# Experts three to thirty-two in an order made on the chip from the token counts, with weight addresses from a table

## The reference, cut to what matters

```python
logits = xt @ w_router + b_router            # 264 tokens, 32 experts
top_val, top_idx = lax.top_k(logits, 4)      # four experts a token
gates = softmax(top_val)
counts = bincount(top_idx)                   # 1056 assignments over 32 experts
for each expert e, each block of its tokens:
    gu  = xb @ w_gate_up[e] + b_gate_up[e]   # 1024 x 2048 weights, 8 MB
    act = (clip(lin) + 1) * min(glu, 7) * sigmoid(1.702 * glu)
    y  += gate * (act @ w_down[e] + b_down[e])   # 1024 x 1024 weights, 4 MB
```

## Time and profile before

| | us |
|---|---|
| median of 3 runs | 1265.24 (1260.77 to 1265.37) |
| profiled execution, first to last instruction (its span) | 1258.5 |
| what lies around the span, median less span | 6.7 |
| PE matmuls busy | 1102.0 (88%) |
| DVE busy | 588.2 (47%) |
| ACT busy | 230.7 (18%) |
| POOL busy | 68.5 (5%) |
| moved by DMA | 485.30 MB, mean 386 GB/s |

### The profile page before, as it was taken

The page is one execution under the profiler, slowest core; times in us unless marked ns, Lnnn a source line. Parts: engine busy times, 40 slices in busy tenths (PEclk is TensorE's granted clock), DMA queues, the critical chain, the costliest instruction groups (busy, mean ns, idle before and its releaser), DMA issues.

```text
span 1258.5 us, 23992 instructions
## 1 busy us (share of the span) xinstructions
PE 1102.0 (88%) x9856; PEld 456.6 (36%) x9856; DVE 588.2 (47%) x1166; ACT 230.7 (18%) x420; POOL 68.5 (5%) x126
## 2 busy tenths in 40 slices
PE   8999999999988697996887979999966995667996
PEld 4776777785322131321222322333211331112332
DVE  3536744444654252563353544666532552332654
ACT  3002510141311110220111211112100211100212
POOL 0312020250100000000000000000000000000000
PEclk9999999999989897998798999999988998888999
DMA  9979994599899999999999999999999999999995
GB/s 342 312 245 347 317 339 154 187 384 366 284 428 429 426 429 426 429 425 429 426 428 428 428 426 393 409 424 427 428 427 428 427 426 430 424 431 425 428 428 236
DMA packets 67619, 485.30 MB, mean 386 GB/s; under 512 B 6421, under 2 KB 29450, under 8 KB 40762
## 3 DMA queue, kind: packets, MB, share of 16 engines
q1 hardware_dynamic: 59312, 461.07, 88.9%
q0 software_dynamic: 7104, 19.65, 4.9%
q10 hardware_dynamic: 1130, 3.51, 0.8%
HBM read 479.47 MB, written 4.72 MB: 385 GB/s over the span
## 4 chain that ended last, share of the span: by engine, by line
DMA 45%; PE 27%; DVE 1%; issue 0%; DVEq 0%; ACT 0%; ACTq 0%
DMA big<-in_w_down 26%; PE PB L1247 13%; DMA big<-in_w_gate_up 13%; PE PB L1274 7%; DMA hTG<-in_w_down 5%; PE PB L1214 2%; PE PB L1201 2%; PE PB L1206 1%; PE PB L1229 1%; PE PB L1221 1%; PE PB L1240 0%; PE PB L1186 0%; PE PB L1232 0%; DVE big L1623 0%; DVE big L1620 0%
## 5 line engine op out<-in xcount | busy, mean ns | idle before, releaser
L1247 PE MATMUL PB<-big,cst 128*32 128x512 f32 x2768 | 355.0, 657 | 109.2 <-DMA big<-in_w_gate_up 109.2
L2189 DVE TENSOR_TENSOR tok<-PB,cst 32x512 f32<-32x512 f32 x188 | 129.1, 687 | 261.7 <-ACT cst L1554 259.8
L1247 PEld LDWEIGHTS PB<-big,cst 128*32 128x32 f32 x2768 | 89.0, 115 | 345.2 <-issue 181.1
L1274 PE MATMUL PB<-big,cst 128*32 128x512 f32 x1408 | 166.6, 602 | 12.8 <-DMA big<-in_w_down 12.7
L2165 DVE TENSOR_SCALAR mod<-PB 64x256 f32<-64x256 f32 x96 | 41.0, 427 | 209.1 <-PE PB L1247 208.4
L756 PE MATMUL PB<-hTG,big 128*128 128x264 f32 x576 | 136.5, 391 | 0.4 <-DVE hTG L1617 0.4
L756 PEld LDWEIGHTS PB<-hTG,big 128*128 128x128 f32 x576 | 106.9, 190 | 27.3 <-issue 10.8
L1544 ACT ACTIVATE mod<-PB 64x256 f32<-64x256 f32 x96 | 36.1, 376 | 422.3 <-PE PB L1247 421.7
L1274 PEld LDWEIGHTS PB<-big,cst 128*32 128x32 f32 x1408 | 39.2, 110 | 96.8 <-issue 65.8
L1201 PE MATMUL PB<-wide,att 128*32 128x256 f32 x784 | 57.9, 415 | 5.1 <-DVE att L2159 4.9
L1554 ACT ACTIVATE cst<-PB 128x512 f32<-128x512 f32 x48 | 28.7, 597 | 178.2 <-PE PB L1274 178.2
(11 more groups left out here) (378 smaller groups left out, 970.9 us busy)
## 6 DMA issues: line engine op xcount, KB each, us to landing
big<-in_w_gate_up SPq DMA_DIRECT2D x115, 2048.0 KB, 31.0
big<-in_w_down SPq DMA_DIRECT2D x57, 2048.0 KB, 23.9
hTG<-in_w_gate_up SPq DMA_DIRECT2D x13, 2048.0 KB, 37.1
big<-in_w_mod SPq DMA_DIRECT2D x24, 1024.0 KB, 7.5
big<-in_w_in SPq DMA_DIRECT2D x22, 1024.0 KB, 9.2
hTG<-in_w_down SPq DMA_DIRECT2D x6, 2048.0 KB, 24.0
wide<-in_cache_k POOLq DMA_DIRECT2D x16, 256.0 KB, 6.8
big<-in_w_out SPq DMA_DIRECT2D x4, 1024.0 KB, 10.5
```

Of the source, the lines that this page charges most:

```text
L1247: mm = pe.matmul(GU[32 * j:32 * j + 32, :], mo["xT"][:, (2 * u + r) * M:(2 * u + r + 1) * M], groups(w[:, r * 2 * D:(r + 1) * 2 * D])[:, j ...
L1274: mm = pe.matmul(DN[32 * j:32 * j + 32, :], mo["actT"][:, (4 * u + r) * M:(4 * u + r + 1) * M], w[:, r * D + half * 512:r * D + (half + 1) ...
L2189: mm = dve.tensor_tensor(mo["y"][rows, :], DN[rows, :], mo["y_part"][other, :], ALU.add)
```

## The change

Experts 0 and 1 stay first. After them the experts are taken in an order which DVE computes: ranked by number of blocks, ties by index, and placed heaviest, lightest, second heaviest, second lightest, and so on (constant `ranks`: 0, 1, 2, 31, 3, 30, ..., 16, 17). `tab` and `used_tab` are rewritten for that order from the third place on, `sel` has its columns exchanged, and the table `order` gives SP the expert at each place. The steps on DVE go ahead of the computation of places. A new semaphore `order_ready` holds SP before unit 12 and PE before the third place. From unit 12 on, SP's transfers take their source address from a register.

```diff
+    pairs = np.stack([np.arange(2, E // 2 + 1), E + 1 - np.arange(2, E // 2 + 1)], 1).reshape(-1)
+    put("ranks", np.tile(np.concatenate([[0, 1], pairs]), (P, 1)))
...
-        tab = sb("tab", [1, E + 2], I32)
-        used_tab = sb("used_tab", [1, E], I32)
+        tables = sb("tables", [33, E + 2], I32)
+        tab, used_tab = tables[0:1, :], tables[32:33, 0:E]
+        order = sb("order", [1, E], I32)
...
+            def load_unit(n, e=None):
+                src = unit_rows(n, slice(n // NU, n // NU + 1) if e is None else bass.ds(e, 1))
                 sp.dma_start(unit_slot(n), src).then_inc(unit_landed(n)[0], 16)
...
             for n in range(NSLOT, NLOAD):
                 e, u = (n - NSLOT) // NU, (n - NSLOT) % NU
+                if n > NSLOT and u == 0:
+                    sp.wait_ge(S("order_ready"), 1)
                 if n == NSLOT or u == 0:
                     before = sp.value_load(used_tab[0:1, e:e + 1], min_val=0, max_val=NU * MAXB)
+                if n // NU >= 2 and n % NU == 0:
+                    sp.wait_ge(S("order_ready"), 1)
+                    expert = sp.value_load(order[0:1, n // NU:n // NU + 1], min_val=0, max_val=E - 1)
                 sp.wait_ge(S("w_used"), before + (u + 1))
-                if n < NLOAD - 1:
+                if n < 2 * NU:
                     load_unit(n)
+                elif n < NLOAD - 1:
+                    load_unit(n, expert)
...
                 if e == 2:
                     down_biases()
+                    pe.wait_ge(S("order_ready"), 1)
...
             dve.nop().then_inc(S("gates_turned"), 1)
-            tt(sv("cmp"), sv("incl"), sv("nb"), ALU.subtract)
+            stt(keys, sv("nb"), 2.0 * E, iota_e, ALU.mult, ALU.subtract)
+            ts(keys[:, 0:2], iota_e[:, 0:2], -1.0, 32.0 * E, ALU.mult, ALU.add)
+            do(dve.transpose(key_of, keys))
+            ts(ahead, keys, key_of[:, 0:1], None, ALU.is_gt)
+            do(dve.tensor_reduce(col[0], ahead, AX, ALU.add))
+            ts(at_place, C("ranks"), col[0], None, ALU.is_equal)
+            tt(spots, at_place, iota_e, ALU.mult)
+            do(dve.tensor_reduce(col[1], spots, AX, ALU.add))
+            copy(spots, col[1].to_broadcast([P, E]))
+            do(dve.transpose(spot_row, spots))
+            stt(weighed, spot_row, col[1], sv("nb"), ALU.is_lt, ALU.mult)
+            do(dve.tensor_reduce(col[2], weighed, AX, ALU.add))
+            copy(spots, col[2].to_broadcast([P, E]))
+            do(dve.transpose(sv("cmp"), spots))
+            do(dve.transpose(at_expert, at_place))
+            tt(weighed, at_expert, iota_e, ALU.mult)
+            do(dve.tensor_reduce(col[3], weighed, AX, ALU.add))
+            copy(spots, col[3].to_broadcast([P, E]))
+            do(dve.transpose(order_row, spots))
+            copy(order[0:1, :], order_row[0:1, :])
+            tt(weighed, at_expert, sv("nb"), ALU.mult)
+            do(dve.tensor_reduce(col[4], weighed, AX, ALU.add))
+            copy(spots, col[4].to_broadcast([P, E]))
+            do(dve.transpose(blocks_row, spots))
+            do(dve.tensor_tensor_scan(sv("incl"), C("ones")[:, 0:E], blocks_row, 0.0, ALU.mult, ALU.add))
+            copy(tab[0:1, 3:E], sv("incl", 2, E - 1, rows=1))
+            ts(used_tab[0:1, 2:E], sv("incl", 2, E, rows=33, r0=32), -1.0, float(NU), ALU.add, ALU.mult)
+            dve.wait_ge(S("sel_ready"), 3)
+            copy(sel[:, 2:E], at_place[0:96, 2:E])
+            dve.nop().then_inc(S("order_ready"), 1)
             dve.wait_ge(S("samples_act"), 7)
```

More of the change, by code:

```diff
@@ L59 @@
                 ("steps", 9), ("slot", 1), ("causal", 128), ("bias", H * 384), ("scan", T),
-                ("sbias", PAST + 1), ("pair", 32), ("selt", NS), ("maps", 2), ("lamc", 2), ("valid", 2)]
+                ("sbias", PAST + 1), ("pair", 32), ("selt", NS), ("maps", 2), ("lamc", 2), ("valid", 2), ("ranks", E)]
 CONST = {}
@@ L402, in _, with unit_rows @@
             win = a["w_in"][0].rearrange("(k p) n -> p k n", p=P)
-            def load_unit(n):
-                e, u = n // NU, n % NU
+            def unit_rows(n, e):
+                u = n % NU
                 if u < 4:
-                    src = a["w_gate_up"][0, e, u * 2 * P:(u + 1) * 2 * P, :].rearrange("(p r) n -> p (r n)", r=2)
-                else:
-                    src = a["w_down"][0, e, (u - 4) * 4 * P:(u - 3) * 4 * P, :].rearrange("(p r) n -> p (r n)", r=4)
+                    return a["w_gate_up"][0, e, u * 2 * P:(u + 1) * 2 * P, :].rearrange("a (p r) n -> p (a r n)", r=2)
+                return a["w_down"][0, e, (u - 4) * 4 * P:(u - 3) * 4 * P, :].rearrange("a (p r) n -> p (a r n)", r=4)
+            def load_unit(n, e=None):
+                src = unit_rows(n, slice(n // NU, n // NU + 1) if e is None else bass.ds(e, 1))
                 sp.dma_start(unit_slot(n), src).then_inc(unit_landed(n)[0], 16)
@@ L479, in _ @@
                 e, u = (n - NSLOT) // NU, (n - NSLOT) % NU
+                if n > NSLOT and u == 0:
+                    sp.wait_ge(S("order_ready"), 1)
                 if n == NSLOT or u == 0:
                     before = sp.value_load(used_tab[0:1, e:e + 1], min_val=0, max_val=NU * MAXB)
+                if n // NU >= 2 and n % NU == 0:
+                    sp.wait_ge(S("order_ready"), 1)
+                    expert = sp.value_load(order[0:1, n // NU:n // NU + 1], min_val=0, max_val=E - 1)
                 sp.wait_ge(S("w_used"), before + (u + 1))
-                if n < NLOAD - 1:
+                if n < 2 * NU:
                     load_unit(n)
+                elif n < NLOAD - 1:
+                    load_unit(n, expert)
                 else:
-                    src = a["w_down"][0, E - 1, 4 * P:8 * P, :].rearrange("(p r) n -> p (r n)", r=4)
+                    src = unit_rows(n, bass.ds(expert, 1))
                     for i, (r0, r1) in enumerate(LAST_ROWS):
@@ L2124, in _ @@
             ts(tab[0:1, E + 1:E + 2], sv("incl", E - 1, E, rows=1), -1.0, None, ALU.add)
-            ts(used_tab[0:1, :], sv("incl", rows=1), -1.0, float(NU), ALU.add, ALU.mult)
+            ts(used_tab[0:1, :], sv("incl", rows=33, r0=32), -1.0, float(NU), ALU.add, ALU.mult)
             dve.nop().then_inc(S("tab_ready"), 1)
@@ L2130, in _, with scratch @@
             dve.nop().then_inc(S("gates_turned"), 1)
-            tt(sv("cmp"), sv("incl"), sv("nb"), ALU.subtract)
+            def scratch(i):
+                return mo["eq"][:, E * i:E * (i + 1)]
+            keys, key_of, ahead, at_place, at_expert, spots, spot_row, weighed, order_row, blocks_row = (
+                scratch(i) for i in range(10))
+            col = [mo["eq"][:, 10 * E + i:10 * E + i + 1] for i in range(5)]
+            iota_e = C("iota_e")
+            stt(keys, sv("nb"), 2.0 * E, iota_e, ALU.mult, ALU.subtract)
[28 more added lines that the diff above has]
+            dve.nop().then_inc(S("order_ready"), 1)
             dve.wait_ge(S("samples_act"), 7)
```

## The result

The changed kernel takes 1276.51 us (median of 4 runs, 1273.04 to 1284.70) against 1265.30 us (1260.77 to 1265.66): a ratio of **1.0119, 95% interval 1.0087 to 1.0151**. It is slower by 1.2%; 1278.2 us had been forecast.

What follows compares the result with a forecast made beforehand. Transfers were taken to bound the kernel, only an empty queue costing time. Unit 22 flowing 17.1 us later, less 4.1 us won, gave +13.0 us: 1265.2 to 1278.2 us, range 1270 to 1286.

Steps and rivals of the forecast that it cites:

- DVE's steps: Serial stretch before the first block's gather: 28 small instructions in, one out, 6.8 us, all delaying PE's first block.
- SP's wait before unit 12: SP waits for the order before issuing unit 12; queued transfers last to about 351 us, so no cost.
- The gap at the head: Transfer queue ahead of unit 14: empty for 5 us, flowing at 366.5 against 361.5 us.
- Rival D: PE's clock stays low after longer idling; up to 14 us more at the third place, 1285 to 1292 us; chance 0.06.
- The third place: Three-block expert holds slots, so unit 22 is issued at 416.0 us and the queue is empty some 12 us.
- What the order gives: The 4.1 us lost at 780 to 790 us go; alternating two-block and one-block experts then causes no stall.
- The sum: Whole kernel: 17.1 us later flow of unit 22 less 4.1 us won, +13.0 us.
- A: At unit 22: the ring takes up the head's delay, only 4.1 us are won, 1261 us; chance 0.05.
- B: At the third place: the hold costs only 4 to 5 us, as at 786; +5, 1270 us; chance 0.11.
- C: SP's issues with register addresses are slow, over 4.9 us each; at 6 us, 1476 us; chance 0.03.
- SP's longest wait: Sign on SP: a wait near 45 us, ending in an issue near 416 us.
- 6.7 us around the span: Difference between profiled span and median, taken as before and added to the 1271.5 us span to give 1278.2 us.

Runs made afterwards that it cites:

- e5: Changed kernel with the first 25 of DVE's 28 new steps done twice; 938.6 us from unit 10's issue to the end, ratio 1.0156 to the kernel before.
- e6: Kernel before with the changed order written in as constants, no DVE steps, waits or register addresses; stretch 925.4 us, ratio 1.0064 to the kernel before.
- e1: Changed kernel with its order undone to 0 to 31, all added steps, waits and register addresses kept; stretch 924.5 us, ratio 1.0043 to the kernel before.
- e8: Changed kernel with the lightest and heaviest experts moved to the last two places, heaviest last; stretch 950.2 us, ratio 1.0260 to the kernel before.
- e3: Changed kernel with the heaviest and lightest experts moved to the seventeenth and eighteenth place; stretch 923.5 us, ratio 1.0035 to the kernel before.
- e4: Changed kernel with its first pair exchanged, lightest expert third and heaviest fourth; stretch 922.9 us, ratio 1.0046 to the kernel before.
- e7: Kernel before with a constant order, lightest third and heaviest fourth, no DVE steps, waits or register addresses; stretch 919.2 us, ratio 0.9997 to the kernel before.
- e2: Changed kernel with index order and SP's transfer addresses fixed again, the steps kept; stretch 923.7 us, ratio 1.0024 to the kernel before.
- run 35: Not a label but a count: the unchanged kernel before was run 35 times for the experiments, with a median of 1260.45 us.

## Why the prediction was right

**The bound.** The transfers bound the experts' part, and only an empty queue costs time: shown by e5 (5.9 us on DVE and 0.75 on PE, 6.6 at the end), by e6 (the order alone, by which unit 22 is issued later) and by the two gaps of the changed kernel.

**DVE's steps.** 6.8 us were taken, 6.36 came (6.59 less the subtraction removed). What the path pays is start to start, 0.235 us, with the wait of each step for its own semaphore in it; the busy times, 0.17 to 0.25 us, sum to 5.5. The estimate from the Trainium skill ("VectorE: DVE Perf Modes", TRN2 errata), 5.3 us, is near that sum, with 0.19 us measured for each tensor_tensor at N = 32, and short of what the path pays.

**SP's wait before unit 12.** It was to cost nothing. Unit 12 was issued at 352.54, 346.6 on the clock of before, and from 353 to 362 the DMA moved 435 GB/s, so it cost nothing.

**The gap at the head.** 5 us forecast, 4.1 measured. PE's first gather was to come near 356.5; on the clock of before it came at 362.05 - 5.98 = 356.1. The third place began only 5.5 us later against unit 10, in place of 6.8: DVE was 0.4 us shorter, and PE left its lower clock sooner within the first block's rest (the prompt scatter, 2.09 us before, took 1.29). That the clock rose sooner is no effect of the change: with the same idle of 11.2 to 11.3 us the scatter took 2.09 us in e1 and e8, 1.75 in e3 and 1.27 in e4. Rival D is refuted, since the longer idle never cost more than the 2.09 us of before, and the blocks at the third place follow each other by 14.5 us as elsewhere. D was also priced too low: two blocks at half speed would add 29 us, not 14.

**The third place.** 12 us forecast, 12.1 measured. Unit 22 was to be issued 35.8 us later than before; it was 75.1 - 40.5 = 34.6. The window from 421 to 424 moved 202 GB/s, 1.4 us of full rate, so the flow began at 422.6, 1.7 us after the issue at 420.85; 1.8 was taken.

**What the order gives.** 4.1 us were booked as won, since they left 780 to 790. By the landings only 2.7 us were lost there. And the wording promised too much: the hold belongs to the expert and goes where it goes. e7 shows that the best place tried gives back nothing, e1 and e3 that by the rate it costs 4.2 and 4.4 us in the middle too.

**The sum.** In its own terms it was 17.1 - 4.1 = 13.0. Measured, unit 22 flowed at 422.6 - 5.98 = 416.6 in place of 400.7, 15.9 us later, and 2.7 were won: 13.2, the whole of the difference. The first term was 1.2 us too high, for DVE's 0.4 and the scatter's 0.8, and the second 1.4 too high. That they cancel is luck; the mechanism is not. e6 bears the 2.7 out: its unit 22, flowing 1.8 us behind its issue, comes 9.6 us later than before, and less 2.7 that is 6.9, where 6.6 were measured and 4.1 would give 5.5.

**The rivals.** A (the ring takes up the delay) needed the last block at the third place to start before 400.8; it started at 418.93, 12 us too late even on the clock of before (412.95). B (the hold costs no more than at 786) is what happens at the fourth place, not at the third. C (slow register addresses) is refuted by e2.

**What was off.** I expected SP's longest wait near 45 us; it is 33.9, because unit 21 was itself issued late, at 385.78, which the forecast had left at its old time. And I put 6.7 us around the span: the profiled executions show 1.7 (1279.4 against 1277.7), so the execution traced before was among the quick ones. A quick run of the changed kernel was then to take 1258.5 + 13.0 + 1.7 = 1273.2 us; its quickest took 1273.04. The agreement of 1278.2 with the median of 1276.51 is thus partly luck: the forecast started from a median of 1265.2, and the same kernel, run 35 and 21 times for the experiments, has medians of 1260.45 and 1260.18.

No version here beats the kernel before. The one gap left in the middle of its transfers is the hold, 4.1 us by the rate and 2.7 by the landings. No order tried removes it for less than it costs: with the heaviest last, 29 us more of PE work stand behind the last landing (e8). A shorter hold would need an eleventh slot or fewer blocks for that expert; neither was tried.

## What to carry to other kernels

With a ring of buffers that a job keeps until its last pass, look at how far the consumer is behind when a long job comes. Right after a start with a full ring it is behind by all that was preloaded, and a job with extra passes then empties the queue for a good part of them (12 of 29 us here), while behind one short job it costs about 3 us.

If transfers already run at full rate everywhere but in one gap, an order can win at most that gap, so price the gap first, by what the consumer waits for and not by the mean rate (2.7 us and not 4.1 here). Then price the steps that compute the order: 28 dependent small instructions take 6.6 us, of which 4.9 reached the end in the index order (e2) and all of it with the heaviest expert third (932.0 against the 925.4 of e6).

## What the runs showed of the hardware that I had not expected

The first part, the same instructions in every kernel here, took from 338.5 to 345.9 us to the issue of unit 10 in different executions. That spread of 7 us is larger than most effects of this study. It goes with the moment at which PE's granted clock first reaches the higher level (2.4 GHz): the traces have it at 11.9 to 21.1 us in the seven executions that took 338.5 to 341.7, and at 30.1 to 32.9 in the three that took 344.5 to 345.9. Before, it is at 16.9, in the changed kernel at 30.8. Between 17 and 30 us, PE busy for 12 us in both, the same matmuls took 390 ns before and 644 in the changed kernel:

```profile
L756 PE MATMUL PB<-hTG,big 128*128 128x264 f32 x24 | 5.6, 390 | 0.4 <-DVE hTG L1617 0.4
```
```profile
L770 PE MATMUL PB<-hTG,big 128*128 128x264 f32 x3 | 1.5, 644 | 0.0
```

Why it rises at such different times, PE having done the same work until then, no run here shows. The three late ones are kernels with register addresses, but three others with such addresses are among the early ones. A yardstick that begins behind this part leaves the spread out. How much it varies by itself is not shown, with one profile of each kernel; the scatter above shows that 0.8 us can differ by the clock alone.

The 16 steps of a transfer drift apart in a full queue and are drawn together by a gap: 5.2 us at 787 in the kernel before, 1.0 behind the hold, and 8.7 us at the end of e7. So the gap at 780 to 790 cost 2.7 us in landings, where the mean rate says 4.1.

A transfer whose address comes from a register is issued by SP as fast as one with a fixed address (1.72 us from issue to issue in both). Over 180 transfers the two kernels differ by 0.8 us in the stretch and 1.5 in the median, not told from zero.
